# Three gate projections of a decoder step by seven block products instead of eight, on sums of weight and token blocks

## What is computed

```python
proj = jnp.einsum('btd,de->bte', u, w_in)
q, k, v, g, p, ga, gb = jnp.split(proj, IN_SPLITS, axis=-1)
...
ya = jnp.einsum('btc,cd->btd', jax.nn.silu(g) * o, w_ret_branch)
...
yb = jnp.einsum('btc,cd->btd', pooled, w_pool_branch)
merged = jax.nn.sigmoid(ga) * ya + jax.nn.sigmoid(gb) * yb
return jnp.einsum('btd,de->bte', merged, w_out), S_new.astype(S0.dtype), pool_new
```

## Time and profile before

| | before |
|---|---|
| median of three runs | 1201.95 us |
| span of the profiled execution | 1198.7 us |
| busy: PE | 1153.0 us (96%) |
| busy: DVE | 307.3 us (26%) |
| busy: ACT | 159.5 us (13%) |
| busy: POOL | 64.8 us (5%) |
| DMA, mean over the span | 380 GB/s |
| mean granted TensorE clock | 0.992 of full |

### The profile page before, as it was taken

How to read it: one execution, slowest core, us unless ns; L and a number is a source line. 1 busy time by engine, 2 the same in 40 slices (tenths; PEclk the granted TensorE clock), 3 DMA queues, 4 the chain that set the end, 5 groups by cost and what they waited for, 6 DMA issues and landing times.

```text
span 1198.7 us, 13664 instructions
## 1 busy us (share of the span) xinstructions
PE 1153.0 (96%) x5403; PEld 571.6 (48%) x5403; DVE 307.3 (26%) x699; ACT 159.5 (13%) x314; POOL 64.8 (5%) x93
## 2 busy tenths in 40 slices
PE   9999999999999999999989998989999989899997
PEld 7888788885534334333434333434333333333332
DVE  4363511232222122222212221213121212121222
ACT  2122111002011111111010101010101101010112
POOL 3252600000000000000000000000000000000000
PEclk9999999999999999999999999999999999999999
DMA  9762788477999999999999999999999999999996
GB/s 321 233 227 91 261 324 322 144 315 280 422 423 428 427 432 429 426 430 431 419 434 427 435 426 432 423 432 426 434 426 432 423 431 429 433 426 428 429 420 252
DMA packets 63728, 455.09 MB, mean 380 GB/s; under 512 B 4321, under 2 KB 35501, under 8 KB 42688
## 3 DMA queue, kind: packets, MB, share of 16 engines
q1 hardware_dynamic: 59168, 439.60, 88.4%
q0 software_dynamic: 4176, 14.34, 3.5%
q10 hardware_dynamic: 344, 0.61, 0.1%
HBM read 448.65 MB, written 6.11 MB: 379 GB/s over the span
## 4 chain that ended last, share of the span: by engine, by line
PE 70%; DMA 27%; SPq 2%; issue 0%; DVE 0%; ACT 0%; POOL 0%; DVEq 0%; ACTq 0%; POOLq 0%
PE psum L1090 25%; PE psum L1019 19%; DMA ring<-in_w_down 18%; PE psum L1101 11%; DMA ring<-in_w_gate_up 8%; PE psum L1177 5%; SPq L591 2%; PE psum L1211 2%; PE psum L1157 1%; PE psum L1167 1%; PE psum L1212 1%; PE psum L1186 1%; DMA ring<-in_w_in 0%; PE psum L1091 0%; PE psum L900 0%
## 5 line engine op out<-in xcount | busy, mean ns | idle before, releaser
L1090 PE MATMUL psum<-ring,x_T 128*64 128x512 f32 x1004 | 456.0, 600 | 10.1 <-DMA ring<-in_w_gate_up 9.3
L1091 PE MATMUL psum<-ring,x_T 128*64 128x512 f32 x994 | 450.9, 600 | 0.0
L1090 PEld LDWEIGHTS psum<-ring,x_T 128*64 128x64 f32 x1004 | 130.8, 137 | 276.0 <-issue 252.2
L1101 PE MATMUL psum<-ring,act_T 128*64 128x512 f32 x960 | 215.7, 602 | 24.0 <-DMA ring<-in_w_down 24.0
L1019 PE MATMUL psum<-ring 128*128 128x264 f32 (+1 forms) x768 | 181.7, 392 | 0.6 <-DMA ring<-in_w_in 0.6
L1019 PEld LDWEIGHTS psum<-ring 128*128 128x128 f32 x768 | 143.2, 190 | 30.2 <-ACT qk L1448 2.1
L1101 PEld LDWEIGHTS psum<-ring,act_T 128*64 128x64 f32 x960 | 70.0, 138 | 157.9 <-issue 138.9
L1091 PEld LDWEIGHTS psum<-ring,x_T 128*64 128x64 f32 x994 | 129.4, 137 | 0.0
L1909 DVE TENSOR_TENSOR h_raw<-psum,params 128x512 f32<-128x512 f32 x32 | 22.1, 692 | 295.3 <-PE psum L1157 295.3
L1926 DVE TENSOR_TENSOR z_T<-z_T,psum 128x264 f32<-128x264 f32 x112 | 43.1, 426 | 205.7 <-PE psum L1212 205.7
L1177 PE MATMUL psum<-normed,one_hot 128*128 128x512 f32 x168 | 74.4, 592 | 0.0
(11 more groups left out here) (270 smaller groups left out, 777.9 us busy)
## 6 DMA issues: line engine op xcount, KB each, us to landing
ring<-in_w_gate_up SPq DMA_DIRECT2D x32, 4096.0 KB, 31.7
ring<-in_w_gate_up SPq DMA_DIRECT2D x59, 2048.0 KB, 28.7
ring<-in_w_down SPq DMA_DIRECT2D x56, 2048.0 KB, 33.3
ring<-in_w_in SPq DMA_DIRECT2D x21, 1024.0 KB, 7.3
ring<-in_w_down SPq DMA_DIRECT2D x12, 1024.0 KB, 27.3
spare<-in_w_gate_up SPq DMA_DIRECT2D x5, 1280.0 KB, 37.0
out<-ring POOLq DMA_DIRECT2D x9, 512.0 KB, 9.4
ring<-in_state_ret POOLq DMA_DIRECT2D x8, 512.0 KB, 7.5
```

The costliest lines, as they stand in the source:

```text
L1090: mm(psum[0:CAP, 2 * j + n], x, gate, start=first, stop=final)
L1091: last = mm(psum[CAP:P, 2 * j + n], x, up, start=first, stop=final)
L1101: last = mm(psum[j * CAP:(j + 1) * CAP, 4 + n], hidden[:, j, 4 * h + i], w, start=h == 0 and i == 0, stop=h == 1 and i == 3)
```

## The change

Two neighbouring tiles (a "group" of 256 columns, one chunk of weights) are now computed together, as a 2 x 2 by 2 x 2 block product: the 1024 rows of the weights are cut in halves of 512, the 256 columns in halves of 128, the 264 tokens in halves of 132. The eight block products become seven (numbered 1 to 7), some of them on sums of blocks. A product is 4 matmuls of 132 columns. There are 12 groups.

- Sums of token blocks: three tensors `x_sums`, made once by DVE before tile 0, and one sum written over a part of u_T behind tile 19.
- Sums of weight blocks, for each group: two by POOL (`weight_sums`, each 128 x 512, the second over the weights themselves), two by DVE (`more_sums`, each 128 x 512), which wait for POOL's.
- Products 1, 6, 5, 3 of a group add up in one PSUM bank; between them DVE copies the partial sum out (`keep_first`, `keep_second`, `keep_third`: each a copy of 128 x 132) and adds product 2, 7 or 4 to the copy. Products 3 and 4 of a group run among those of the next.
- ACT applies the gate's function at once to one quarter from PSUM and to three quarters in SBUF.
- The extra work moves to other places and banks: "o" 0 and 1 into group 0, `next_state` in pairs behind groups 2, 3, 6 and 7, `read_state` in pairs behind groups 4, 5, 7 and 8; the group norm of the running tokens is split, its first part at group 8, its second (`o_s_ready`) at group 9.
- SP loads three expert chunks instead of four ahead of the pool branch, the fourth behind the second chunk of the retention branch.

```diff
+GROUPS = (N_IN - G0) // 2
+PRODUCTS = []
+for _g in range(GROUPS):
+    PRODUCTS += [(_g, 1), (_g, 2)] + [(_g - 1, 3)] * (_g > 0) + [(_g, 6), (_g, 7)] + [(_g - 1, 4)] * (_g > 0) + [(_g, 5)]
...
+STATES_NEXT = {2: (0, 1), 3: (2, 3), 6: (4, 5), 7: (6, 7)}
+STATES_READ = {4: (0, 1), 5: (2, 3), 7: (4, 5), 8: (6, 7)}
+FEW_NORM_AT = 9
...
             sp.wait_ge(o_s_ready, 1)
-            for s in range(NS):
-                sp.wait_ge(state_out[s], 16)
+            sp.wait_ge(states_out, 16 * NS)
             sp.wait_ge(stored, 16 * 3)
-            for s in range(4):
+            for s in range(3):
                 load_chunk(sp, 0, 0, s)
             for i in range(C_PB, len(CHUNKS)):
...
             pool.wait_ge(aux_took, AUX_AT[("o", 1)] + 1)
             nc.gpsimd.memset(both_squares, 0.0).then_inc(zeroed, 1)
+            weight_sums(3)
             for b in range(4):
+                if b == 2:
+                    weight_sums(4)
                 pool.wait_ge(state_ready, b + 1)
                 spread_row(b + 4)
+            weight_sums(5)
             for b in range(4, NS):
                 rank_one(b)
+                if b % 2 == 1:
+                    weight_sums(6 + b // 2 - 2)
             for b in range(NS):
+                if b == 6:
...
+            for g in range(9, GROUPS):
+                weight_sums(g)
...
+            def product(g, i):
+
+                w, sums, low, high = group_chunk(g), w_sums[g % 2], slice(0, HK), slice(HK, KD)
+                total, other, extra = SUM_BANK[g % 2], OTHER_BANK, EXTRA_BANK[g % 2]
+                if i == 1:
+                    wait_group_chunk(pe, g)
+                    if g < 2:
+                        pe.wait_ge(act_took, G0 - 2 + g + 1)
+                    else:
+                        pe.wait_ge(c12_taken, g - 1)
+                    bank, a, x = total, w[:, low, 0:P], u_T[:, low, 0:HALF]
+                elif i == 2:
+                    if g > 0:
+                        pe.wait_ge(quarter_ready, QUARTER_AT[g - 1, 11])
+                    bank, a, x = other, w[:, high, 0:P], u_T[:, high, 0:HALF]
+                elif i == 6:
+                    if g == 0:
+                        pe.wait_ge(x_sums_ready, 4)
+                    pe.wait_ge(parts_kept, 3 * g + 1)
+                    pe.wait_ge(w_more_ready, 2 * g + 1)
+                    bank, a, x = total, sums[:, 0], x_sums[:, 1]
+                elif i == 7:
+                    if g == 1:
+                        pe.wait_ge(aux_took, AUX_AT[("o", 0)] + 1)
+                    elif g > 1:
+                        pe.wait_ge(quarter_ready, QUARTER_AT[g - 2, 21])
+                    pe.wait_ge(w_two_ready, 2 * g + 1)
+                    bank, a, x = extra, sums[:, 1], u_T[:, low, HALF:NT]
+                elif i == 5:
+                    pe.wait_ge(parts_kept, 3 * g + 2)
+                    pe.wait_ge(w_two_ready, 2 * g + 2)
+                    bank, a, x = total, w[:, low, P:2 * P], x_sums[:, 0]
+                elif i == 3:
+                    pe.wait_ge(parts_kept, 3 * g + 3)
+                    pe.wait_ge(w_more_ready, 2 * g + 2)
+                    bank, a, x = total, sums[:, 2], u_T[:, high, HALF:NT]
+                else:
+                    pe.wait_ge(quarter_ready, QUARTER_AT[g, 22])
+                    bank, a, x = extra, w[:, high, P:2 * P], x_sums[:, 2]
+                for k in range(HK):
+                    last = mm(psum[:, bank, 0:HALF], a[:, k], x[:, k], start=k == 0 and i in (1, 2, 7),
+                              stop=k == HK - 1, skip_group_check=i not in (1, 2, 7))
+                last.then_inc(product_done, 1)
...
+                for g in range(GROUPS):
+                    product(g, 1)
+                    product(g, 2)
+                    if g == 0:
+                        aux(("o", 0))
+                    else:
+                        product(g - 1, 3)
+                    product(g, 6)
+                    product(g, 7)
+                    if g == 0:
+                        aux(("o", 1))
+                    else:
+                        product(g - 1, 4)
+                    product(g, 5)
+                    if g > 0:
+                        for a in AUX_AFTER[G0 + 2 * g]:
+                            aux(a)
+                    for b in STATES_READ.get(g, ()):
...
+            def more_sums(g):
+
+                w, sums = group_chunk(g), w_sums[g % 2]
+                dve.wait_ge(w_two_ready, 2 * g + 2)
+                if g > 1:
+                    dve.wait_ge(product_done, PRODUCT_AT[g - 2, 6])
+                V.tensor_tensor(sums[:, 0], w[:, 0:HK, P:2 * P], w[:, 0:HK, 0:P], ALU.subtract).then_inc(w_more_ready, 1)
+                dve.wait_ge(w_more_ready, 2 * g + 1)
+                if g > 1:
+                    dve.wait_ge(product_done, PRODUCT_AT[g - 2, 3])
+                V.tensor_tensor(sums[:, 2], w[:, HK:KD, 0:P], sums[:, 0], ALU.subtract).then_inc(w_more_ready, 1)
+
+            def keep_first(g):
+
+                c11 = group_gates(g)[:, 0, 0:HALF]
+                dve.wait_ge(product_done, PRODUCT_AT[g, 1])
+                V.tensor_copy(c11, psum[:, SUM_BANK[g % 2], 0:HALF]).then_inc(parts_kept, 1)
+                dve.wait_ge(product_done, PRODUCT_AT[g, 2])
+                dve.wait_ge(parts_kept, 3 * g + 1)
+                V.tensor_tensor(c11, psum[:, OTHER_BANK, 0:HALF], c11, ALU.add).then_inc(quarter_ready, 1)
+
+            def keep_second(g):
+
+                dve.wait_ge(product_done, PRODUCT_AT[g, 6])
+                V.tensor_copy(group_gates(g)[:, 1, 0:HALF], psum[:, SUM_BANK[g % 2], 0:HALF]).then_inc(parts_kept, 1)
+
+            def finish_second(g):
+
+                c21 = group_gates(g)[:, 1, 0:HALF]
+                dve.wait_ge(parts_kept, 3 * g + 2)
+                dve.wait_ge(product_done, PRODUCT_AT[g, 4])
+                V.tensor_tensor(c21, psum[:, EXTRA_BANK[g % 2], 0:HALF], c21, ALU.add).then_inc(quarter_ready, 1)
+
+            def keep_third(g):
+
+                c22 = group_gates(g)[:, 1, HALF:NT]
+                dve.wait_ge(product_done, PRODUCT_AT[g, 5])
+                V.tensor_copy(c22, psum[:, SUM_BANK[g % 2], 0:HALF]).then_inc(parts_kept, 1)
+                dve.wait_ge(parts_kept, 3 * g + 3)
+                V.tensor_tensor(c22, psum[:, EXTRA_BANK[g % 2], 0:HALF], c22, ALU.add).then_inc(quarter_ready, 1)
+
...
+                for g in range(GROUPS):
+                    keep_first(g)
+                    if g + 1 < GROUPS:
+                        more_sums(g + 1)
+                    if g == 0:
+                        dve.wait_ge(aux_done, AUX_AT[("o", 0)] + 1)
+                        norm_stats(banks(AUX_BANKS[("o", 0)][0], 2), H)
+                    keep_second(g)
+                    if g == 0:
+                        aux(("o", 0))
+                        dve.wait_ge(aux_done, AUX_AT[("o", 1)] + 1)
+                        norm_stats(banks(AUX_BANKS[("o", 1)][0], 2), H)
+                    else:
+                        if g == 1:
+                            aux(("o", 1))
+                        finish_second(g - 1)
+                    keep_third(g)
+                    if g > 0:
+                        for a in AUX_AFTER[G0 + 2 * g]:
+                            aux(a)
+                    for b in STATES_NEXT.get(g, ()):
+                        next_state(b)
+                    if g + 1 == FEW_NORM_AT:
+                        dve.wait_ge(outer_read, NS)
+                        norm_stats(psum[:, 7, 0:DV], 1)
+                    if g == FEW_NORM_AT:
+                        norm_apply(2, psum[:, 7, 0:DV], 1).then_inc(o_s_ready, 1)
+                finish_second(GROUPS - 1)
```

More of the change, by code:

```diff
@@ L970, in turn_roots @@
                 pe.transpose(psum[:, 3, 384:384 + 28], rows[0:28, 0:P], ident[0:28, 0:28]).then_inc(params_turned, 1)
-            for n in range(T_END):
-                if n >= 3:
+            for n in (*range(G0), *range(N_IN, T_END)):
+                if n == T_POOL:
+                    gate_groups()
+                if n == T_YB:
+                    product(GROUPS - 1, 3)
+                    product(GROUPS - 1, 4)
+                if 3 <= n < G0 or n >= T_YB + 3:
                     wait_taken(pe, n - 3)
```

203 lines of the change are left out of this document (149 added, 54 removed).

## The result

| | kernel before | changed kernel |
|---|---|---|
| median of the runs | 1202.01 us | 1225.87 us (4 runs, 1225.76 to 1226.62) |
| ratio, 95% interval | | 1.0199 [1.0187, 1.0211] |
| profiled span | 1198.7 us | 1224.1 us |
| pool branch starts on PE | 198.50 us | 221.77 us |
| first retention tile | 212.74 us | 237.95 us |

A forecast was written before the change was run, and what follows sets the result against it. PE's gate stage bounds the kernel, with the pool-branch weight chunk just under it. Terms -9.5 - 0.8 + 17.8 + 4.5 = +12.0 us on the 1198.7 span, median 3.25 above: 1214.0 us, range 1198 to 1222.

The forecast's parts named there:

- The price of a product, 0.90 us: PE, gate stage: eight records of 132 columns at 0.113 us each make a product 0.90 us.
- rival 3: PE's matmuls: narrow matmuls pay their weight loads, 0.163 us a record instead of 0.113; +30 us, 1232 us, chance 0.04.
- the places of the seven holes: PE, gate stage: waits before product 6 in groups 3, 4, 7 and before product 5 in groups 3, 4, 7, 8.
- Rivals 1 and 2: Gate stage: waits hide; 1, chunk does not, 1199 us, chance 0.20; 2, chunk in time, 1192 us, chance 0.11.
- rival 1's second chunk time: SP's queue: the last store, issued around 165 us and landing 12.1 later, holds the pool-branch chunk until 197.6 us.
- +17.8 of waits: PE, gate stage: waits for DVE's copies, 5.2 us for states plus 12.6 for late POOL and small waits.
- +4.5: Pool branch start: its chunk, behind `o_s_ready`, lands at 210.5 us while PE could start at 206.0.
- the forecast's own holes: PE: 17.4 us of gate-stage holes without the small waits, and 4.5 us for the pool-branch chunk.
- The 5.2 us for the states: Before product 6: `next_state` ahead of `keep_first` makes PE wait 2.0, 2.0 and 1.2 us in groups 3, 4, 7.
- the 12.6 for GpSimd: Before product 5: late POOL sums cost 1.7, 3.5, 1.8, 5.2 us in groups 3, 4, 7, 8, plus 0.4 small.
- the 3.5 us for product 5 of group 4: PE, group 4: product 5 waits 3.5 us for late POOL weight sums, with two more states first.
- the right paragraph: POOL's new work: a two-SBUF-input DVE instruction waits for POOL's to end, up to 1.1 us each meeting.

The follow-up runs named there:

- the fastest kernel: The 1199.01 us kernel with one more GpSimd wait: rank-one products of states 6 and 7 wait for VectorE's group 6 sums; 1197.52 us, 0.9963.
- the kernel without that order: Changed kernel with only the second state update of each pair moved behind `keep_first` of the next group; 1231.14 us, 1.0233.
- the wait alone: Changed kernel with one more GpSimd wait: rank-one products of states 4 to 7 start after VectorE's group 5 sums; 1223.97 us, 1.0182.
- the last two kernels: The 1203.85 us kernel with GpSimd waits on VectorE's sums, without and with the wait for states 6 and 7; 1199.01 and 1197.52 us.
- 1203.85: Changed kernel with pool-branch chunk asked for early, GpSimd's sums ahead of state waits, and second state updates moved behind `keep_first`; 1203.85 us, 1.0014.
- 1199.01: The 1203.85 us kernel plus GpSimd waits for VectorE's sums: before its own sums and before rank-one products of states 4 and 5; 1199.01 us, 0.9970.
- 1210.65 us: Kernel before with one wait: PE stands ahead of gate tile 34 until GpSimd has cleared a small region ten times; 1210.65 us, 1.0063.
- the kernel of 1212.40 us: Changed kernel with GpSimd's weight sums for groups 4, 5, 8 and 9 moved ahead of the waits for states; 1212.40 us, 1.0088.

## Why the prediction was wrong

**What held.** The price of a product, 0.90 us; that weight loads are hidden (rival 3 is out, by the 0.90 us and by the fastest kernel, which needs 193.75 - 93.81 = 99.9 us from its first product to the pool branch, 3.4 of them holes, where the 24 tiles took 104.85); the places of the seven holes, their sum to 0.5 us (single ones by up to 1.7); `o_s_ready` 1.8 us behind group 10's start (1.9 forecast; group 10 itself started at 198.5 instead of 188.4); a chunk 21.3 us behind it (20.2 forecast); an expert stage as long as before. Rivals 1 and 2 both had the waits hidden, and fell with the holes. Two small sums of the prediction don't close: along its timeline the pool branch starts at 188.4 + 17.4 = 205.8 us, not 206.0, and rival 1's second chunk time is 165 + 12.1 + 20.2 = 197.3, not 197.6; neither changes anything.

**The step that failed** is "+17.8 of waits" and "+4.5", as the two entered the sum: each hole was charged its own length, and all of PE's work around it at 0.2225 and 0.113 us a record. These durations are from a stretch with the clock at 1.00 and no hole; the kernel of the forecast had 18 us of holes, and no row of before could show what work behind a hole costs. It costs 7.6 us in the gate stage and 1.9 in the pool branch here; 1.64 and 2.55 us behind single holes of 2.67 and 5.45 us in the kernel before. The clock is the larger part of the 13.25 us; the rest is the later start, the chunk, 0.5 us of holes and the restarts, as listed above, and 1.45 us went the other way, as the median lay 1.8 us above the span and not 3.25. With half of each hole added, the forecast's own holes (17.4, and the 4.5 us for the chunk) would have given 11 us more, 1225; that this comes so near is partly luck, for the half clock made 9.5 of it. The forecast also had no case in which holes cost more than they last, so the range ended too low, at 1222.

**Right sum, partly wrong cause.** That the holes add up to 18.35 us, for 17.8, is in part luck. The 5.2 us for the states stood beside the 12.6 for GpSimd like a term of its own; before products 6 they measured 1.70 + 1.66 + 0.90 = 4.3 us, but VectorE waits for GpSimd's sums longer than that right behind them, and the kernel without that order was slower, not faster. Both terms hang on one thing, when GpSimd gets through its queue. And the 3.5 us for product 5 of group 4 were put down to GpSimd's late sums; it measured 5.21, and 5.21 - 1.95 = 3.3 of it were the hold by the rank-one products, which the forecast had in the right paragraph and not at the right place.

## What to carry to other kernels

A wait that takes the place of work on TensorE can cost more than its length. Behind every hole of 2.67 us or more in these kernels the clock fell, and in the two that were measured alone this cost about half the hole again; with holes of about 2 us it fell in one execution and not in another, so there a forecast needs a range. Look whether harmless matmuls can fill the hole. Holes that two engines cause are not a sum: find the engine whose queue sets the last of them, and try the removal of each alone. When work is given to GpSimd and VectorE together, place the long GpSimd operations by what VectorE does at that time; one wait on GpSimd for VectorE's short sums took 3 to 5 us out of one hole. Other holes grew in turn: by the medians the kernels gained 1.9 us (the wait alone), 4.8 and 1.5 us (the last two kernels).

## What was not expected of the hardware

- The length of a hole alone doesn't tell whether the clock falls. It fell to 1.2 GHz at the hole of 1.97 us in the changed kernel, with another of 1.70 us and 3.0 us of work ahead of it. In the kernel of 1223.97 us the same two holes with the same work between them left it at 1.00, and so did one of 2.17 us that brought it down in the changed kernel. It did not fall behind single holes of 1.77, 1.70, 1.66, 1.38 and 0.90 us.
- It also fell without any hole. In three kernels (1203.85, 1199.01 and 1210.65 us) the 24 transposes of the routing, behind short small matmuls, took 4.48 us instead of 2.82, in all others 2.82, and no edit touches them. The first row is from the kernel of 1203.85 us, where the granted clock from 276 to 279 us is 0.52; the second is from the changed kernel, with 1.00. Differences of 1.7 us between two of these kernels can be this alone. What decides it, no run here shows.

```profile
275.47 4.48 PE L1210 MATMUL psum<-consts,z_T 128*128 128x128 f32 x24
```

```profile
299.16 2.82 PE L1210 MATMUL psum<-consts,z_T 128*128 128x128 f32 x24
```

- One DVE subtraction was held for 5.07 us beyond its 0.68, through three GpSimd instructions; one in the kernel of 1212.40 us took 5.86.
